# Two heads in a slot: a reordered prompt mixer of a hybrid decoder step on one Trainium2 core

## The reference, cut to what matters

```
A:  lg = q . k * 64**-0.5 ; lg = -inf where the key is not chosen ; out = softmax(lg) @ v
B:  S = diag(f_t) S + (1 - f_t) i_t^T ; o_t = S^T q_t
    o = rmsnorm(o) * silu(gate)
```

## Time and profile before

| | us |
|---|---|
| median of 3 runs | 3404.92 |
| lowest, highest | 3403.15, 3412.81 |
| the profiled execution, its own time | 3405.46 |
| its span in the trace | 3403.3 |
| TensorE, VectorE, ScalarE, GpSimd busy | 3095.3, 1714.4, 799.1, 488.4 |

### The profile page before, as it was taken

How to read it: one execution, slowest core, us unless ns; L and a number is a source line. 1 busy time by engine, 2 the same in 40 slices (tenths; PEclk the granted TensorE clock), 3 DMA queues, 4 the chain that set the end, 5 groups by cost and what they waited for, 6 DMA issues and landing times. The chain is left out here.

```text
span 3403.3 us, 42176 instructions
## 1 busy us (share of the span) xinstructions
PE 3095.3 (91%) x17344; PEld 2632.4 (77%) x17344; DVE 1714.4 (50%) x2105; ACT 799.1 (23%) x1206; POOL 488.4 (14%) x498
## 2 busy tenths in 40 slices
PE   6889999996869997999999999996399999999988
PEld 3584444675247775899999999995299999999988
DVE  2169993799156554344333343555743433334454
ACT  2231135333135541221111111231131111111232
POOL 1424334434533212100000000000000000000000
PEclk8899999998889997999999999998799999999999
DMA  2251110432641103111111111010011111111011
GB/s 87 71 161 42 72 55 29 142 115 91 182 123 32 32 14 107 61 50 39 50 50 42 47 50 48 19 55 25 25 55 49 50 44 44 50 38 51 25 51 65
DMA packets 160172, 207.63 MB, mean 61 GB/s; under 512 B 17062, under 2 KB 121038, under 8 KB 159965
## 3 DMA queue, kind: packets, MB, share of 16 engines
q1 hardware_dynamic: 144869, 154.24, 14.1%
q0 software_dynamic: 15104, 50.47, 5.0%
HBM read 182.13 MB, written 22.78 MB: 60 GB/s over the span
## 5 line engine op out<-in xcount | busy, mean ns | idle before, releaser
L1944 PE MATMUL ps<-h_split,w_split 128*128 128x352 f32 x7488 | 1216.3, 324 | 17.2 <-DVE w_split L2414 8.2
L1944 PEld LDWEIGHTS ps<-h_split,w_split 128*128 128x128 f32 x7488 | 1206.6, 189 | 24.3 <-issue 12.1
L1944 PE MATMUL ps<-hidden,w_split 128*128 128x352 f32 x3456 | 566.2, 323 | 0.0
L1944 PEld LDWEIGHTS ps<-hidden,w_split 128*128 128x128 f32 x3456 | 558.1, 188 | 0.0
L428 PE MATMUL ps<-w_chunk,hT 128*128 128x512 f32 (+3 forms) x1008 | 400.9, 552 | 26.9 <-DMA w_chunk<-in_w_in 26.9
L428 PEld LDWEIGHTS ps<-w_chunk,hT 128*128 128x128 f32 (+1 forms) x1008 | 169.6, 183 | 231.6 <-issue 199.5
L2452 DVE TENSOR_TENSOR xT<-xT,ps 128x1056 f32<-128x1056 f32 x176 | 220.5, 1253 | 203.0 <-PE ps L1944 202.8
L2431 DVE TENSOR_TENSOR hT<-hT,ps 128x1056 f32<-128x1056 f32 x44 | 55.0, 1254 | 361.8 <-PE ps L1944 361.8
L2305 ACT CAST w_split<-hT 128x2048 fp32r<-128x2048 f32 (+1 forms) x82 | 145.3, 1772 | 388.2 <-PE ps L1944 388.2
L2414 DVE TENSOR_TENSOR w_split<-hT,w_split 128x2048 fp32r<-128x2048 f32 (+1 forms) x82 | 175.0, 2134 | 80.4 <-ACT w_split L2305 79.3
L736 DVE TENSOR_SCALAR_CACHE_REDUCE score_hits<-xT,threshold 128x384 uint8<-128x384 f32 (+2 forms) x198 | 174.2, 943 | 3.2
(11 more groups left out here) (336 smaller groups left out, 3320.1 us busy)
## 6 DMA issues: line engine op xcount, KB each, us to landing
hT<-in_w_up SPq DMA_DIRECT2D x44, 1024.0 KB, 5.2
hT<-in_w_down SPq DMA_DIRECT2D x22, 1024.0 KB, 4.9
w_chunk<-in_w_in SPq DMA_DIRECT2D x6, 2048.0 KB, 8.5
hT<-in_w_ple_gate SPq DMA_DIRECT2D x16, 512.0 KB, 3.9
x_rows<-in_x_prompt SPq DMA_DIRECT2D x8, 512.0 KB, 4.6
w_gate_tile<-in_w_in SPq DMA_DIRECT2D x8, 512.0 KB, 4.4
w_out_raw<-in_w_out SPq DMA_DIRECT2D x8, 512.0 KB, 4.4
x_rows<-in_x_prompt SPq DMA_DIRECT2D x16, 256.0 KB, 2.8
```

Of the source, the lines that this page charges most:

```text
L1944: m = pe.matmul(out, w[a], x[b][:, g * GC:(g + 1) * GC], start=first and i == 0, stop=last and i == 2)
```

## The change

1. A tile of the prompt mix has four slots instead of eight. A slot works two heads and two levels. The scores of the next pair are issued part by part, the two heads in turn (array rows 0 to 63 and 64 to 127, each head in banks of its own); the value products of the pair before are issued head by head, all of the first head and then all of the second. The probabilities of two pairs lie in the upper half of xT, where only the sample states lay.
2. Scores have four banks. B's small products have one (SIDE) instead of three: keys, read-out, state update, inverse sums and output transposes use it one after the other. So ScalarE copies the read-out to SBUF (`on`) after it has squared it, `update` waits for this copy, `read_out` for `out_copied`, and `turn_ke` for `mixed` (the product at L1083).
3. The order on each engine is written anew: the first transposes of a pair stand ahead of the next scores, `update` in the second slot, `turn_inv` and `spread_inv` in the third, `turn_ke` and `turn_out` in the fourth; the normalising of B ends the third slot of VectorE, attention's product follows in the fourth after two maskings and a placing. `copy_out` of a tile comes a tile later on ScalarE.
4. The first two maskings come ahead of most of the memsets. The first level no longer waits for the constants: the first placing waits for the level masks alone (`l_landed`), the first normalising for the other three.
5. The sample states are loaded after the last transposes of A, because they share the memory of the probabilities.
6. In the sample stage the four scans of the gates stand behind the sample softmax on VectorE.

The core of the diff:

```
-    @block.vector
-    def _(dve):
+    def scan_gates(dve):
         dve.wait_ge(const_landed, 16)
...
+    k.scan_gates = scan_gates
...
+            k.scan_gates(dve)
             dve.wait_ge(v_landed, 32)
...
-    tiles, SLOTS = NT + 1, LEVELS + 1
-    steps = [(i, h) for i in range(NT) for h in range(H)]
+    tiles, SLOTS = NT + 1, H // 2
+    steps = [(i, f) for i in range(NT) for f in range(SLOTS)]
...
-    SCORE, TURNED, WEIGHED, PROD, SIDE, OUT, UPD = 0, 2, 3, 4, 5, 6, 7
+    SCORE, TURNED, WEIGHED, PROD, SIDE = 0, 4, 5, 6, 7
...
+        sp.wait_ge(turned, turns)
+        sp.dma_start(s0, io["state_glr"][0].rearrange("b h d v -> d b h v")).then_inc(s0_landed, 16)
...
             for a in range(parts(u)):
                 cols = part_cols(u, a)
+                for e in range(2):
+                    row = e * DH
+                    m = pe.matmul(ps[:, score_bank(u, e) + a, 0:cols.stop - cols.start],
+                                  k.qT[row:row + DH, f, i * P:(i + 1) * P], k.kT[row:row + DH, f, cols], start=True, stop=True)
...
+            for e in range(2):
+                for j in range(i + 1):
+                    row, h = e * DH, 2 * f + e
+                    m = pe.matmul(ps[row:row + DH, WEIGHED, f * P:(f + 1) * P], v[:, j, h * DH:(h + 1) * DH],
+                                  probT[:, u % 2, e, j, :], start=j == 0, stop=j == i)
...
         def turn_ke(c):
             pe.wait_ge(qe_made, c + 1)
+            if c:
+                pe.wait_ge(mixed, c)
...
         def update(c):
-            pe.wait_ge(ke_copied, c + 1)
+            pe.wait_ge(out_kept, c + 1)
```

TensorE's order in a slot f of tile c, u being the pair:

```
+                if pair:
+                    turn(u, 0, 0)
+                if u + 1 < len(steps):
+                    score(u + 1)
+                if pair and wide(u):
+                    turn(u, 0, 1)
+                if c and f == 0:
+                    read_out(c - 1)
+                if c and f == 1:
+                    update(c - 1)
+                if c and f == 2:
+                    turn_inv(c - 1)
+                if (c, 2 * f) in nth_product:
+                    product(c, 2 * f)
+                if pair:
+                    turn(u, 1, 0)
+                if f == 3:
+                    turn_ke(c)
                 if 0 < u <= len(steps):
                     weigh(u - 1)
+                if c and f == 2:
+                    spread_inv(c - 1)
+                if pair and wide(u):
+                    turn(u, 1, 1)
+                if (c, 2 * f + 1) in nth_product:
+                    product(c, 2 * f + 1)
+                if c and f == 3:
                     turn_out(c - 1)
```

and VectorE's:

```
+                if (c, 2 * f + 1) in nth_level:
+                    scale_level(nth_level[c, 2 * f + 1])
                 if u + 1 < len(steps):
+                    bias(u + 1, 0)
+                if (c, 2 * f) in nth_product:
+                    place(c, 2 * f)
+                if u + 1 < len(steps):
+                    bias(u + 1, 1)
+                if c and f == 1:
                     update_state(c - 1)
+                if c and f == 3:
+                    normalise_att(c - 1)
+                following = (c, 2 * f + 2) if f < 3 else (c + 1, 0)
+                if following in nth_level:
...
+                    scale_level(nth_level[following])
+                if f == 2:
+                    edges(c)
+                if (c, 2 * f + 1) in nth_product:
+                    place(c, 2 * f + 1)
+                if c and f == 1:
                     mean(c - 1)
                     invert(c - 1)
+                if c and f == 2:
                     normalise(c - 1)
```

More of the change, by code:

```diff
@@ L845, in parts, with nth_part @@
         return 2 if wide(u) else 1
-    def parts_before(u):
-        return sum(parts(x) for x in range(u))
+    def nth_part(u, e, a):
+        return sum(2 * parts(x) for x in range(u)) + e * parts(u) + a
     def part_cols(u, a):
@@ L852, in part_cols, with score_bank, scores @@
         return slice(512 * a, min(w, 512 * (a + 1)))
-    def score_bank(u):
-        return SCORE if wide(u) else SCORE + u % 2
-    def scores(u):
+    def score_bank(u, e):
+        return SCORE + 2 * e if wide(u) else SCORE + 2 * (u % 2) + e
+    def scores(u, e):
         w = (steps[u][0] + 1) * P
-        at = score_bank(u)
+        at = score_bank(u, e)
         return ps[:, at:at + parts(u), :].rearrange("p b n -> p (b n)")[:, 0:w]
+    turns = sum(2 * parts(u) for u in range(len(steps)))
     def halves(ap, w):
@@ L950, in spread_inv @@
             for f in range(4):
-                m = pe.matmul(ps[:, UPD, f * P:(f + 1) * P], heads[:, f, :], invT[:], start=True, stop=True)
+                m = pe.matmul(ps[:, SIDE, f * P:(f + 1) * P], heads[:, f, :], invT[:], start=True, stop=True)
             m.then_inc(spread, 1)
@@ L1220, in _ @@
+                if c == NT and f == 3:
+                    split_values(0)
+                    split_values(1)
+                    decay_samples(0)
+                    decay_samples(1)
         for h in range(BH):
@@ L1255, in copy_inv @@
                 act.wait_ge(spread, i)
[L1256 removed]
+            act.copy(invT[:], ps[0:H, SIDE, 0:P]).then_inc(inv_copied, 1)
         def exp_dif(e):
@@ L1290, in copy_out @@
             act.copy(mixT[:, BH:2 * BH, c * P:c * P + n], src[:, :, 0:n]).then_inc(out_copied, 1)
+        exp(0, 0)
+        exp(0, 1)
         exp_dif(0)
         exp_dif(1)
-        exp(0)
         for c in range(tiles):
-            for i in range(SLOTS):
-                u = SLOTS * c + i
-                ahead = {LEVELS - 2: (c + 1, 0), LEVELS: (c + 1, 1)}.get(i, (c, i + 2))
-                if ahead in nth_level and i != LEVELS - 1:
-                    exp_dif(nth_level[ahead])
-                if u < len(steps):
-                    copy(u, 0)
+            for f in range(SLOTS):
+                u = SLOTS * c + f
+                pair = u < len(steps)
+                if c >= 2 and f == 0:
+                    copy_out(c - 2)
+                if pair:
+                    copy(u, 0, 0)
+                following = (c, 2 * f + 2) if f < 3 else (c + 1, 0)
+                if following in nth_level:
+                    exp_dif(nth_level[following])
+                if pair and wide(u):
+                    copy(u, 0, 1)
+                if c and f == 0:
+                    square(c - 1)
+                if c and f == 2:
+                    copy_inv(c - 1)
+                if pair:
+                    copy(u, 1, 0)
+                if f == 3:
+                    copy_ke(c)
                 if u + 1 < len(steps):
-                    exp(u + 1)
-                if i == 0 and c:
+                    exp(u + 1, 0)
+                if c and f == 0:
                     copy_att(c - 1)
-                if i == 1 and c:
-                    square(c - 1)
-                if i == 2:
-                    exp_edges(c)
-                if i == 3 and c:
-                    copy_inv(c - 1)
-                if i == 5:
-                    copy_ke(c)
-                if u < len(steps) and wide(u):
-                    copy(u, 1)
-                if i == 7 and c:
-                    copy_out(c - 1)
+                if u + 1 < len(steps):
+                    exp(u + 1, 1)
+                if pair and wide(u):
+                    copy(u, 1, 1)
+                following = (c, 2 * f + 3) if f < 3 else (c + 1, 1)
+                if f != 2 and following in nth_level:
+                    exp_dif(nth_level[following])
+                if f == 1:
+                    exp_edges(c)
+        copy_out(NT - 1)
         square(NT)
@@ L1359, in _ @@
                 edge(0)
-            if c == NT and i == 0:
-                pass
             make_dif(e)
-            if c and c < NT and i == 4:
+            if c and c < NT and i == 5:
                 rstd(c - 1)
```

186 lines of the change are left out of this document (74 added, 112 removed).

## The result

The changed kernel takes **3373.2 us** (median of 4 runs, 3369.5 to 3376.6) beside 3404.5 of the kernel before on the same chip: ratio 0.9903, 95% interval 0.9883 to 0.9922, 31 us less. The forecast was 3357, the range 3335 to 3392; the rival *value products one after the other* had given 3374. In the profiled executions the prompt mix loses 22.4 us (from its first memset to the next stage's first transpose 374.7 us, then 352.3) and the stretch before it 6.9; the prediction had put 39 and 9.

What follows compares the result with a forecast made beforehand. TensorE's own work was taken to bound the wide tiles, a TensorE-VectorE loop the narrow ones. From 3405.5 us, -8.7 - 9.5 - 42.5 + 6 + 13.5 - 17 + 7 + 3 = -48 gave 3357 us, range 3335 to 3392.

Steps and rivals of the forecast that it cites:

- value products one after the other: Rival: column halves of the value products don't overlap, or only at the seam of two heads; 3374 us, chance 0.32.
- value products, -17: Prompt mix: two heads' value products overlap on column halves though issued head by head; 15 us in tiles 4-7, 2 in 2-3.
- Scores, -31: Prompt mix: a pair's scores run side by side on row halves, saving half of 62 us of TensorE's work.
- The -11.5 for the changes of form: Prompt mix, TensorE: the array changes form 32 times fewer for scores and for values, saving 11.5 us.
- The stall at the keys, +13.5: Prompt mix: turn_ke waits for VectorE's normalised attention, so TensorE stands some 2.7 us in each of five tiles; 13.5 us lost.
- the +6: Tiles 0 to 2: VectorE's order sets the time, so 6 of their 9.6 us of TensorE savings are given back.
- Clock, +7: Prompt mix: seven stalls at turn_ke each bring 3.5 us at the lower clock, costing 7 us more than before.
- the rival in which the clock eats the gain: Rival: TensorE stays at 1.2 GHz for half of each of tiles 1 to 7; slower, 3423 us, chance 0.06.
- Start, -9.5: Start of the prompt mix: the first placing waits for the level masks alone and comes 9.5 us earlier.
- Scans, -8.7: Sample stage: scans behind the softmax start the chain to the value products 10.1 us earlier, less 1.4 for slower gathers.
- Tail, +3: End of the prompt mix: one bank puts in a row what ran side by side; 3 us lost, 0 to 6.
- that cover: Tail: work ahead of the sample states' first reader lasts longer than their load's 12.3 us, so the later load costs nothing.

Runs made afterwards that it cites:

- in turn: Changed kernel with a pair's value products alternating between the two heads block by block, instead of head by head: 3358.5 us.
- the early product: Changed kernel with VectorE's normalising product moved ahead of the placing and the second head's masked score of its slot: 3354.9 us.
- all three repairs: Changed kernel with value products alternating between heads, the keys' turn behind them on TensorE, and VectorE's normalising product moved earlier: 3340.5 us.
- the inverse ahead: The kernel with all three repairs, and besides VectorE's inverse of the totals put ahead of the means of the outputs: 3344.1 us.
- the table alone: Kernel before, with only the table of levels given its own semaphore and other small constants waited for at first use: 3399.5 us.

## Why the prediction was right, and where it was not

The sign, the range and most steps held; the forecast is 16 us too low. One term is missing, worth 14.7 us when it is put right. That the rest of the sum then comes out within 2 us is in part luck: measured alone, three other terms were too large by some 13 us together (see the start and the scans below).

**Failed: value products, -17.** I took the side of the earlier trace rows: "where the first head's four passes also stand ahead of the second's in the program and still ran beside them". What carried over from there was not the order but the distance. A pass overtakes three waiting passes of the other half, so a run of four overlaps with the next, a run of eight in part, one of sixteen only at its seam: 3.26 us, where 32 passes of 0.107 each in a row and the change of form would be 3.6, so three passes. The term was next to nothing in the wide tiles: 0.3 us a pair in tile 7, where half would have been 1.7. That the halves can run side by side was right, and worth 14.7 us, near the 17, in an order that the change does not have. The prediction named this outcome, "only at the seam of two heads", as a rival with a chance of 0.32, and its 3374 us is what was measured. The Trainium skill's rule of parallel tiles ("TensorEngine Tiling (Array Packing)", Key Properties) held in turn, at 1.89 us; the rule of program order ("TensorE: Matmul & The Clock Gate", Part 3) comes near the runs of sixteen, though there too the second head's first pass starts ahead of three of the first head's, and neither says how far apart partners may stand.

**Scores, -31: right in kind,** 1.92 us for eight passes; worth 25.2 when undone; the waits that shrink by 11.2 us then are room enough for the rest. The -11.5 for the changes of form was not tried by itself.

**The stall at the keys, +13.5 for five tiles at 2.7: right in its cause, lucky in its size.** Tiles 4 to 6 waited 2.71, 2.65 and 2.59 us, and the narrow tiles 3.7 to 3.9, which the +6 had to hold. But the 2.7 was worked out for tile 7's width, and tile 7 waited only 1.17. Undone from VectorE's side it gave 18.3 with its clock, where the three terms for it and for the clock made 26.5.

**Clock, +7: right in number, in part by luck.** Seven short falls in the tiles, and no long one; the rival in which the clock eats the gain had nothing for it. But the seven that were counted were the stalls at the keys, and only five of the falls came at these; the stalls of tiles 4 and 7 (2.71 and 1.17 us) brought none, and two falls came at other waits. With the wait made shorter by the early product the falls went from seven to three, with all three repairs to none between 961 and 1200 us, and with the inverse ahead back to three, though the wait for the keys was shorter still. So the stalls at the keys set off most of the falls of the changed kernel, but not they alone decide. The prediction's "twice in this stage" holds for the tiles alone: in the kernel before the clock also fell in the tail, from 1273 and from 1293.5 us.

**Start, -9.5: right at the first placing (10.2), wrong at the end.** The first tile moves into a stretch at the lower clock, 7 us of it here and 16 in the kernel with the table alone, where it was worth 5.1. **Scans, -8.7:** -6.0 alone, at the upper bound I gave. So these two moves and the scores brought less than forecast, by some 13 us if what they are worth alone adds up (2.7, 4.4 and 5.8; each has an interval of 3 to 8 us to either side). If so, other terms must have brought as much more, for without the values the sum ended on 3374; which ones, the changes of form, the narrow tiles or the stalls' price, the runs don't tell.

**Tail, +3:** from the last turn (1227.4) to the start of the last copy (1280.0) it takes 52.6 us, from 1264.4 to 1309.2 before it was 44.8. Of the 7.8 us some 3.1 are products that now lie behind the last turn: about +5, inside the range of 0 to +6. TensorE's rows show the chain of one bank:

```profile
1244.95 1.01 PE L984 MATMUL ps<-ident,g_ke 128*32 128x128 f32 x4 [3.50 <-DVE hT L1095]
1246.72 1.08 PE L992 MATMUL ps<-ident,g_on 128*128 128x128 f32 x4 [0.76 <-ACT g_ker L1311]
1248.79 0.60 PE L1009 MATMUL ps<-g_val,g_att 32*32 32x128 f32 x2 [0.98 <-ACT hT L1317]
```

The keys wait 3.50 us for VectorE, the norm's turn 0.76 for ScalarE's copy, the read-out 0.98 for another. The sample states landed at about 1240.9, ahead of the read-out at 1248.79; that cover held.

## What to carry to other kernels

Before counting on two halves of the array side by side, look in the issue order how many passes of one half stand in a row ahead of the other's, and interleave them in runs of four or fewer: here a pass overtook three waiting ones and no more. When several small products are put into one bank, write down for each engine what stands ahead of the instruction that frees it: here one line of VectorE's order, moved up by two instructions, was worth 18 us, more than half of what the change gained. Work that is only moved earlier can land in a stretch of lower clock, and then its gain is to be counted less.

## What was not expected of the hardware

Passes on two halves of the array, rows or columns, ran side by side though not neighbours in the order: 1.89 us for 32 value passes in runs of two, 1.95 in runs of four, 2.50 in runs of eight, 3.26 in runs of sixteen. The starts in the traces show the distance: a pass of one half overtook up to three waiting passes of the other, and never a fourth. Why it is three the runs don't show.

The clock fell within a microsecond of the end of waits of TensorE as short as 1.75 us, and tile 4's wait of 2.71 us in the same kernel had no fall. With the wait for the keys at 0.4 to 1.0 us (the early product alone) there was none in tiles 4 to 7, though the turns of the probabilities there waited up to 1.9 us for ScalarE. So the length of a single wait did not tell whether the clock fell. And the lower level at the start of the stage did not move with the work: it ended 2 us behind the first placing in the kernel before, 7 in the changed one and 15.5 in the one with the table alone; what sets that the runs don't show.
